# Latent attention on one core: two heads of a pair share one value product in the column halves of TensorE's array

## The chip, the cores and the metric

One core of a Trainium2 chip runs the whole program. A core has TensorE (matrix products, called PE in the profile, its weight loads PEld), VectorE (DVE), ScalarE (ACT), GpSimd (POOL) and SyncE (SP, which issues the weight DMAs); each works through its own queue in order and waits for the others on semaphores. SBUF is the working memory, PSUM the memory of eight banks that TensorE writes. The metric is the device time of one execution in microseconds (us), as a median of the runs.

## The reference

Two transformer blocks of the same sequence follow one another: a block with a feed-forward layer, a hybrid mixer and another feed-forward layer, and a second block of two layers with a recurrent mixer and a window attention. The change touches one part only, the latent attention of the mixer. It has 8 heads, 512 tokens and 16 meta tokens, and for every block of 128 queries only the keys up to its own block are used:

```python
def latent_attention(q_nope, q_rope, k_nope, k_rope, v, cid):
    scale = (MLA_NOPE + MLA_ROPE) ** -0.5
    outs = []
    for blk in range(lp // Q_BLOCK):
        q0, q1 = blk * Q_BLOCK, (blk + 1) * Q_BLOCK
        kend = min(lp, chunk_end(q1 - 1))
...
        s = s.astype(jnp.float32) * scale
        mask = cid[None, :kend] <= cid[q0:q1, None]
        p = jax.nn.softmax(jnp.where(mask, s, NEG_INF), axis=-1)
        outs.append(jnp.einsum('bhts,bhsd->bhtd', p.astype(v.dtype), v[:, :, :kend]))
    return jnp.concatenate(outs, axis=2)
```

A head's query and key have 96 elements, its value 64.

## The kernel before

The program is a list of stages; between some of them (`phase_end`) TensorE, ScalarE and VectorE wait for one another. `s_latent` is one stage. It interleaves two works that have nothing to do with each other: the latent attention, and the 16 gate projections that the mixer needs later.

**Units.** The attention is cut into `NU` = 32 units of one head and one block of 128 queries. Unit u has i + 1 blocks of 128 keys (called n = i + 1 below, 1 to 4) and the 16 meta keys. Before the change the order is head, then query block, so n runs 1, 2, 3, 4, 1, 2, 3, 4. For each unit:

- `scores` (TensorE, L1578 and L1579): one product for the n key blocks, one for the meta keys, into one of two PSUM areas (`sbank`); it waits until the exponent of the unit two before has read that area.
- `top` (VectorE, L1641, L1643, L1647): masks a corner, takes the row maximum and scales it.
- exponent (ScalarE, L1692) from PSUM into `pm`, with the row sum; two buffers.
- `norm` (VectorE, L1652, L1655): reciprocal of the sum, and `pm` scaled by it in place.
- `turn` (TensorE, L1588 and L1591): n transposes and one for the meta keys, into PSUM bank 4 and 5.
- `keep` (ScalarE, L1686 and L1687): copies the transposed probabilities into `pT`, two buffers of 640 columns.
- `pv` (TensorE, L1601 and L1603): the value product. The stationary operand is a head's value block, 128 keys by 64, the moving one 128 columns of `pT`; n products and one with the 16 meta keys add up in PSUM bank 6. The result has 64 rows: a head with an even number takes partitions 0 to 63 of the bank, one with an odd number 64 to 127.

**Gate work.** `gate(n)` is one step of a projection: three matmuls of 128 by 128 with 512 columns (L294, L295, L296 in the helper `mm3`). Eight steps fill PSUM bank 7 with one chunk; VectorE then copies it out (L1664) and ScalarE and GpSimd split the next weight chunk (L282, L289). All 16 chunks use bank 7, so the first step of a chunk waits for that copy.

**Order.** It is written out by hand. TensorE's iteration u: `scores(u + 2)`, two gate steps, `turn(u)`, a gate step, `pv(u - 1)`, a gate step. A chunk of the gates takes two iterations, so a new chunk begins in every even iteration, right after `scores`. VectorE's iteration u: `top(u + 1)`, in even ones the gate copy of the chunk that has just ended, `norm(u)`. ScalarE's: exponent of u, `keep(u - 1)`, in even ones a weight split; after both heads of a pair are done it also copies bank 6 into `ym` (L1700), which VectorE completes (L1659).

Most float32 products of the attention show as two records in the trace for one matmul of the program: `pv` of n blocks has 2n records on L1601 and two on L1603. The transposes have one each, and so have the gate steps.

Of the kernel before, what the change touches and what calls it, by code (L numbers as in the profile page):

```python
# [17 lines left out]
ACT = mybir.ActivationFunctionType  # L18
# [3 lines left out]
P = 128  # L22
T = 512
META = 16
# [62 lines left out]
def slot_of(base, k, per_body=RING, j=0):  # L87

    g = base + k
    return g % RING, g // RING + (per_body // RING) * j, g + per_body * j  # L90


def program(nc, d, out):
    with ExitStack() as ctx:
# [9 lines left out]
        def local(kind, **totals):  # L104


            out_ = []
            for i, total in enumerate(totals.values()):
                name = f"{kind}{i}"
                out_.append(Signal(sem(name).s, ends.get(name, 0)))  # L110
                ends[name] = ends.get(name, 0) + total
            return out_
# [4 lines left out]
        def at(name, off, shape, dt=F32):  # L117

            n = 4 * int(np.prod(shape[1:]))
            assert off + n <= 56800 * 4, (name, off, n)  # L120
            return nc.alloc_sbuf_tensor_at(name, shape, dt, offset=base0 + off, align_bytes=4)
# [6 lines left out]
        o_tmp = o_big + 98304  # L128
# [60 lines left out]
        vm = at("vm", B + 32768, [P, 5, 8, 64])  # L189
# [1 line left out]
        km = at("km", B + 79872, [96, 8, TK])  # L191
        ym = at("ym", B + 63488, [P, 4, 2, T], F32R)
        pm = at("pm", o_tmp, [P, 2, TK])
        pT = at("pT", o_tmp + 4224, [P, 2, 640])
        kvf = at("kvf", o_tmp + 9344, [P, 2, TK])
        st = at("st", o_tmp + 13568, [P, 64])
        mixh = at("mixh", X + 1024, [P, DT, T], F32R)
        mixl = at("mixl", X + 1024 + 4 * DT * T, [P, DT, T], F32R)
        f_mix = at("f_mix", B, [P, DT, TK])
# [46 lines left out]
        PS = ctx.enter_context(nc.psum_tensor("PS", [P, 8 * 512], F32))  # L246
        PS3 = PS[:, :].rearrange("p (b n) -> p b n", b=8)
# [5 lines left out]
        def c_(name, lo=0, hi=None, rows=slice(0, P)):  # L253
            return con[rows, COFF[name] + lo:COFF[name] + (dict(CON)[name] if hi is None else hi)]
# [46 lines left out]
        def phase_end(eng, who):  # L301

            bars[who] += 1
            eng.drain().then_inc(phase_over.s, 1)
            eng.wait_ge(*phase_over(3 * bars[who]))
# [136 lines left out]
        def xn_ready(pe, tag, t):  # L442

            if tag in raw_low:
                pe.wait_ge(*raw_low[tag](t + 1))
            else:
                pe.wait_ge(*xn_done[tag][t % 2](t // 2 + 1))
# [1101 lines left out]


        def s_latent():
            units = [(hd, i) for hd in range(8) for i in range(4)]
            NU = len(units)
            SC = float(96) ** -0.5
            s_done, masked, mx_done, nb_done, p_done, rs_done, pn_done, t_done, tc_done, pv_done = local(
                "st", s=NU, mask=NU, mx=NU, nb=NU, p=NU, rs=NU, pn=NU, t=NU, tc=NU, pv=NU)
            y_hi, y_lo = local("su", yhi=4, ylo=4)

            gate_base = BASE["gate"]
# [2 lines left out]
            def width(u):  # L1562
                return P * (units[u][1] + 1) + META

            def sbank(u, a, b, rows=slice(0, P)):
                o = 1024 * (u % 2)
                return PS[rows, o + a:o + b]

            def pe(pe):
                phase_end(pe, "pe")  # L1570

                def scores(u):
                    hd, i = units[u]
                    n = P * (i + 1)
                    if u >= 2:
                        pe.wait_ge(*p_done(u - 1))
                    q = qm[:, hd, i * P:(i + 1) * P]
                    pe.matmul(sbank(u, 0, n), q, km[:, hd, 0:n], start=True, stop=True, skip_group_check=True)  # L1578
                    pe.matmul(sbank(u, n, n + META), q, km[:, hd, T:TK], start=True, stop=True,  # L1579
                              skip_group_check=True).then_inc(s_done.s, 1)  # L1580

                def turn(u):
                    hd, i = units[u]
                    pe.wait_ge(*pn_done(u + 1))
                    if u >= 1:
                        pe.wait_ge(*tc_done(u))
                    for x in range(i + 1):
                        pe.transpose(PS[:, 2048 + x * P:2048 + (x + 1) * P], pm[:, u % 2, x * P:(x + 1) * P],  # L1588
                                  c_("ident"))
                    n = P * (i + 1)  # L1590
                    pe.transpose(PS[0:META, 2560:2560 + P], pm[:, u % 2, n:n + META], c_("ident")).then_inc(t_done.s, 1)  # L1591

                def pv(u):
                    hd, i = units[u]
                    r = 64 * (hd % 2)
                    pe.wait_ge(*tc_done(u + 1))
                    if hd >= 2 and hd % 2 == 0 and i == 0:
                        pe.wait_ge(*y_lo(hd // 2))
                    o = PS3[r:r + 64, 6, i * P:(i + 1) * P]
                    for x in range(i + 1):  # L1600
                        pe.matmul(o, vm[:, x, hd, :], pT[:, u % 2, x * P:(x + 1) * P], start=(x == 0),  # L1601
                                  stop=False, skip_group_check=True)
                    pe.matmul(o, vm[0:META, 4, hd, :], pT[0:META, u % 2, 512:640], start=False, stop=True,  # L1603
                              skip_group_check=True).then_inc(pv_done.s, 1)

                def gate(n):

                    c, kt = divmod(n, DT)
                    s, _, g = slot_of(gate_base, c)
                    if kt == 0:  # L1610
                        pe.wait_ge(*lo_done(g + 1))
                        if c:
                            pe.wait_ge(*gate_out(c))
                    if c == 0:
                        xn_ready(pe, "gx", kt)
                    ins = mm3(pe, PS3[:, 7, :], s, kt * P, (kt + 1) * P, xh512[:, kt, :], xl512[:, kt, :],
                              kt == 0, kt == DT - 1)
                    if kt == DT - 1:
                        ins.then_inc(chunk_used.s, 1)
                scores(0)  # L1620
                scores(1)
                for u in range(NU):
                    if u + 2 < NU:
                        scores(u + 2)
                    gate(4 * u)
                    gate(4 * u + 1)
                    turn(u)
                    gate(4 * u + 2)
                    if u >= 1:
                        pv(u - 1)  # L1630
                    gate(4 * u + 3)
                pv(NU - 1)

            def dve(dve):
                phase_end(dve, "dve")
# [41 lines left out]
            def act(act):  # L1677
                phase_end(act, "act")
                act.preload_act_table_set("natural_log_exp_and_others")

                def keep(u):
                    n = P * (units[u][1] + 1)
                    act.wait_ge(*t_done(u + 1))
                    if u >= 2:
                        act.wait_ge(*pv_done(u - 1))
                    act.activation(pT[0:META, u % 2, 512:640], PS[0:META, 2560:2560 + P], ACT.Copy)  # L1686
                    act.activation(pT[:, u % 2, 0:n], PS[:, 2048:2048 + n], ACT.Copy).then_inc(tc_done.s, 1)  # L1687
                for u in range(NU):
                    act.wait_ge(*nb_done(u + 1))
                    if u >= 2:  # L1690
                        act.wait_ge(*t_done(u - 1))
                    act.activation(pm[:, u % 2, 0:width(u)], sbank(u, 0, width(u)), ACT.Exp,  # L1692
                                   bias=st[:, 4 + u % 4:5 + u % 4], scale=SC,
                                   accum_out=st[:, 8 + u % 4:9 + u % 4]).then_inc(p_done.s, 1)
                    if u >= 1:
                        keep(u - 1)
                    if u % 8 == 1 and u >= 8:
                        pair = u // 8 - 1
                        act.wait_ge(*pv_done(8 * pair + 8))
                        act.activation(ym[:, pair, 0, :], PS3[:, 6, :], ACT.Copy).then_inc(y_hi.s, 1)  # L1700
                    if u % 2 == 0 and u >= 2:
                        split_hi(act, gate_base, u // 2 - 1 + 4)
                keep(NU - 1)
                split_hi(act, gate_base, 15 + 4)
                act.wait_ge(*pv_done(NU))
                act.activation(ym[:, 3, 0, :], PS3[:, 6, :], ACT.Copy).then_inc(y_hi.s, 1)
            sp_, pool_ = weights("gate")
            stage(pe, act, dve, pool_, sp_)
# [1064 lines left out]
        s_c_split()  # L2773
        s_mla_project()
        s_latent()
        led = s_mix()
        parts = s_out("wout", (8,), lambda kt, i: (mixh[:, kt, :], mixl[:, kt, :]), T, 4, led, f_mix)
# [202 lines left out]
```

## Time and profile before

| | us |
|---|---|
| median of 3 runs | 2752.3 |
| lowest, highest run | 2749.68, 2753.54 |
| the profiled execution's own time | 2752.45 |
| its span, first to last instruction | 2750.7 |
| TensorE busy (share of the span) | 2619.9 (95%) |
| VectorE, ScalarE, GpSimd busy | 1301.3, 934.3, 1002.4 |

TensorE's granted clock is 0.978 of full over the span. On the profile's page, the chain of work that ended last lies on TensorE for 84% of the span and on VectorE for 9%. Busy time on TensorE counts modelled ends of pipelined matmuls, which overlap; what a piece of work costs there is better read from the distance between starts. The stage `s_latent` runs from 692.6 to 870.4 us.

### The profile page before, as it was taken

To read this page: it belongs to the slowest core of one execution; us is meant where nothing else is said; L and a number is where in the kernel's file an instruction comes from. 1 tells how busy PE (TensorE), PEld (TensorE's weight loads), DVE (VectorE), ACT (ScalarE), POOL (GpSimd) and SP (SyncE) were. 2 spreads that over 40 slices of the span, in tenths; PEclk is the share of its full clock that TensorE was granted. 3 is DMA by queue.
4 is the path that set the end of the run, shared out by engine and by line. 5 is a ranking of instruction groups with operands and counts; after the bars stand their busy time and mean duration, and the time that the engine had idled before them with its cause. 6 is when DMAs were issued, how large, how long until landed. Compare 5 with 4: busy or idle time off the path is not lost.

```text
span 2750.7 us, 35023 instructions
## 1 busy us (share of the span) xinstructions
PE 2619.9 (95%) x13396; PEld 2145.8 (78%) x13396; DVE 1301.3 (47%) x1448; ACT 934.3 (34%) x1305; POOL 1002.4 (36%) x447
## 2 busy tenths in 40 slices
PE   7999999897999999999899899999999899999999
PEld 7999998755676778888667478888877578888887
DVE  4333113467444544430367576664146655666313
ACT  4222223373334242222344232222245453222223
POOL 4433443202222334444323134444444104444442
PEclk9999999998999999999999999999999999999999
DMA  4222232101111222223222022223322102323232
GB/s 165 91 91 75 85 108 77 48 1 41 46 47 62 79 82 99 92 82 97 83 74 77 16 90 93 99 94 105 100 84 92 46 10 99 99 92 99 100 100 69
DMA packets 65650, 219.37 MB, mean 80 GB/s; under 512 B 8273, under 2 KB 8529, under 8 KB 65426
## 3 DMA queue, kind: packets, MB, share of 16 engines
q1 hardware_dynamic: 63792, 216.60, 24.1%
q10 hardware_dynamic: 1762, 1.45, 0.2%
q8 instruction: 65, 1.06, 0.2%
q14 instruction: 31, 0.25, 0.0%
HBM read 215.92 MB, written 2.10 MB: 79 GB/s over the span
## 4 chain that ended last, share of the span: by engine, by line
PE 84%; DVE 9%; ACT 3%; issue 3%; DMA 0%; DVEq 0%; ACTq 0%; SPq 0%; POOL 0%
PE PS L294 25%; PE PS L296 25%; PE PS L295 25%; PE PS L2635 1%; DVE acc L494 1%; PE PS L1601 1%; ACT xh L468 1%; PE PS L1228 1%; PE PS L1578 1%; DVE h L564 1%; PE PS L2618 1%; DVE mt L1752 1%; DVE xl L472 1%; PE PS L1213 1%; DVE sq L486 0%
## 5 line engine op out<-in xcount | busy, mean ns | idle before, releaser
L289 POOL TENSOR_TENSOR wlo<-wraw,whi 128x1024 fp32r<-128x1024 f32 (+2 forms) x425 | 994.4, 2342 | 1560.6 <-ACT whi L282 1560.3
L294 PE MATMUL PS<-xh,whi 128*128 128x512 f32 (+2 forms) x2536 | 908.5, 358 | 44.5 <-DVE xl L472 20.0
L295 PE MATMUL PS<-xl,whi 128*128 128x512 f32 (+2 forms) x2536 | 894.5, 353 | 0.0
L296 PE MATMUL PS<-xh,wlo 128*128 128x512 f32 (+2 forms) x2536 | 894.4, 353 | 0.0
L282 ACT ACTIVATE whi<-wraw 128x1024 fp32r<-128x1024 f32 (+2 forms) x425 | 428.4, 1009 | 857.8 <-PE PS L296 855.8
L294 PEld LDWEIGHTS PS<-xh,whi 128*128 128x128 f32 (+1 forms) x2536 | 478.8, 189 | 119.0 <-issue 24.6
L296 PEld LDWEIGHTS PS<-xh,wlo 128*128 128x128 f32 (+1 forms) x2536 | 479.1, 189 | 65.7 <-issue 0.5
L295 PEld LDWEIGHTS PS<-xl,whi 128*128 128x128 f32 (+1 forms) x2536 | 479.4, 189 | 61.2 <-issue 1.4
L294 PE MATMUL PS<-hid2h,whi 128*128 128x512 f32 x560 | 217.8, 389 | 0.0
L295 PE MATMUL PS<-hid2l,whi 128*128 128x512 f32 x560 | 217.8, 389 | 0.0
L296 PE MATMUL PS<-hid2h,wlo 128*128 128x512 f32 x560 | 217.8, 389 | 0.0
L295 PEld LDWEIGHTS PS<-hid2l,whi 128*128 128x128 f32 x560 | 105.1, 188 | 22.0
L294 PEld LDWEIGHTS PS<-hid2h,whi 128*128 128x128 f32 x560 | 105.1, 188 | 21.8
L926 DVE TENSOR_TENSOR h<-PS,h 128x512 f32<-128x512 f32 x24 | 16.6, 692 | 222.9 <-PE PS L296 222.9
L296 PEld LDWEIGHTS PS<-hid2h,wlo 128*128 128x128 f32 x560 | 105.1, 188 | 21.7
L998 DVE TENSOR_SCALAR f<-PS 128x528 f32<-128x528 f32 (+1 forms) x16 | 11.2, 700 | 221.1 <-ACT sq L986 200.6
L816 DVE SCALAR_TENSOR_TENSOR gc<-gp,vec,gc 128x512 f32<-128x512 f32 x96 | 112.5, 1229 | 0.0
L295 PE MATMUL PS<-hid1l,whi 128*128 128x264 f32 x352 | 100.3, 285 | 0.0
L296 PE MATMUL PS<-hid1h,wlo 128*128 128x264 f32 x352 | 100.2, 285 | 0.0
L294 PE MATMUL PS<-hid1h,whi 128*128 128x264 f32 x352 | 100.1, 284 | 0.0
L806 DVE TENSOR_TENSOR gp<-PS,rb_up 128x1024 f32<-128x1024 f32 x24 | 29.4, 1224 | 144.8 <-PE PS L296 144.8
L468 ACT ACTIVATE xh<-h,vec 128x512 fp32r<-128x512 f32 (+1 forms) x64 | 45.6, 722 | 151.7 <-DVE h L926 112.4
(414 smaller groups left out, 3311.5 us busy)
## 6 DMA issues: line engine op xcount, KB each, us to landing
wraw<-w_up_dram SPq DMA_DIRECT2D x96, 512.0 KB, 3.4
wraw<-w_dn_dram SPq DMA_DIRECT2D x48, 512.0 KB, 3.4
wraw<-w_f1gu_dram SPq DMA_DIRECT2D x44, 512.0 KB, 3.2
wraw<-w_f2gu_dram SPq DMA_DIRECT2D x44, 512.0 KB, 3.4
wraw<-w_hyin_dram SPq DMA_DIRECT2D x24, 512.0 KB, 3.5
wraw<-w_win_dram SPq DMA_DIRECT2D x18, 512.0 KB, 3.2
wraw<-w_gate_dram SPq DMA_DIRECT2D x16, 512.0 KB, 3.2
wraw<-w_pg_dram SPq DMA_DIRECT2D x16, 512.0 KB, 3.4
```

The costliest lines, as they stand in the source:

```text
L282: act.activation(whi[:, s, 0:size], wraw[:, s, 0:size], ACT.Copy).then_inc(hi_done.s, 1)
L289: pool.tensor_tensor(wlo[:, s, 0:size], wraw[:, s, 0:size], whi[:, s, 0:size].bitcast(F32), ALU.subtract).then_inc(lo_done.s, 1)
L294: pe.matmul(out_, whi[:, s, a:b], xhi, start=start, stop=False, skip_group_check=True)
L295: pe.matmul(out_, whi[:, s, a:b], xlo, start=False, stop=False, skip_group_check=True)
L296: return pe.matmul(out_, wlo[:, s, a:b], xhi, start=False, stop=stop, skip_group_check=True)
L468: act.activation(dh[:, t, 0:n], h[:, t, 0:n], ACT.Copy, scale=v_(gain, t)).then_inc(high.s, 1)
L472: dve.scalar_tensor_tensor(dl[:, t, 0:n], h[:, t, 0:n], v_(gain, t), dh[:, t, 0:n].bitcast(F32), ALU.mult, ALU.subtract).then_inc(low.s, 1)
L494: dve.tensor_tensor(acc[:, 0:n], acc[:, 0:n], sq[:, 0:n], ALU.add).then_inc(summed.s, 1)
L564: dve.tensor_tensor(h[:, t, 0:n], scaled_f[:, t % 2, 0:n], h[:, t, 0:n], ALU.add).then_inc(kept.s, 1)
L806: dve.tensor_tensor(gp[:, :, 2:T + 2], bank(0, 2), spread(rb_up, 1), ALU.mult).then_inc(g_read.s, 1)
L816: ins = dve.scalar_tensor_tensor(gc[:, m, :], gp[:, m, tap:T + tap], vec[:, bass.ds(2 * j + (cw + FF2T * tap + m), 1)], gc[:, m, :], ALU.m ...
L1213: ins = pe.matmul(PS3[0:rows(u), 2 * (u % 3) + hd, c0:T], ks[r:r + 64, p, k0:k1], qs[r:r + 64, p, c0:T], start=True, stop=False, skip_grou ...
```

## The change

Units are ordered pair of heads, query block, head of the pair: n runs 1, 1, 2, 2, 3, 3, 4, 4. The value product `pv(m)` now serves the two units 2m and 2m + 1, which are the two heads of a pair at the same query block. Its matmuls alternate between the heads, so that each one goes to the other half of the array's columns than the one before it: partitions 0 to 63 of bank 6, then 64 to 127. It runs in every second iteration (even u from 2 on) and once at the end. `pT` has four buffers instead of two, and `st` lies further back in memory to make room. The waits and counts on `pv_done` follow; `keep(u)` now waits for the value product of units u - 4 and its pair.

```diff
-            units = [(hd, i) for hd in range(8) for i in range(4)]
+            units = [(2 * p + e, i) for p in range(4) for i in range(4) for e in range(2)]
...
-                def pv(u):
-                    hd, i = units[u]
-                    r = 64 * (hd % 2)
-                    pe.wait_ge(*tc_done(u + 1))
-                    if hd >= 2 and hd % 2 == 0 and i == 0:
-                        pe.wait_ge(*y_lo(hd // 2))
-                    o = PS3[r:r + 64, 6, i * P:(i + 1) * P]
+                def pv(m):
+                    p, i = divmod(m, 4)
+                    pe.wait_ge(*tc_done(2 * m + 2))
+                    if p >= 1 and i == 0:
+                        pe.wait_ge(*y_lo(p))
+
+                    def o(e):
+                        return PS3[64 * e:64 * e + 64, 6, i * P:(i + 1) * P]
                     for x in range(i + 1):
-                        pe.matmul(o, vm[:, x, hd, :], pT[:, u % 2, x * P:(x + 1) * P], start=(x == 0),
-                                  stop=False, skip_group_check=True)
-                    pe.matmul(o, vm[0:META, 4, hd, :], pT[0:META, u % 2, 512:640], start=False, stop=True,
-                              skip_group_check=True).then_inc(pv_done.s, 1)
+                        for e in range(2):
+                            pe.matmul(o(e), vm[:, x, 2 * p + e, :], pT[:, (2 * m + e) % 4, x * P:(x + 1) * P], start=(x == 0),
+                                      stop=False, skip_group_check=True)
+                    for e in range(2):
+                        ins = pe.matmul(o(e), vm[0:META, 4, 2 * p + e, :], pT[0:META, (2 * m + e) % 4, 512:640], start=False,
+                                        stop=True, skip_group_check=True)
+                    ins.then_inc(pv_done.s, 1)
...
-                    if u >= 1:
-                        pv(u - 1)
+                    if u >= 2 and u % 2 == 0:
+                        pv(u // 2 - 1)
                     gate(4 * u + 3)
-                pv(NU - 1)
+                pv(NU // 2 - 1)
...
-                    if u >= 2:
-                        act.wait_ge(*pv_done(u - 1))
+                    if u >= 4:
+                        act.wait_ge(*pv_done(u // 2 - 1))
```

TensorE, value products, before: the end of iteration 3 and a part of iteration 4, with value products in both (`xh_56`, `xl_57` and `whi`, `wlo` are the gate steps' operands, `pT` and `vm` those of the value product).

```order
L294 MATMUL PS<-xh_56,whi 128x512
L295 MATMUL PS<-xl_57,whi 128x512
L296 MATMUL PS<-xh_56,wlo 128x512
L1601 MATMUL PS<-pT,vm 64x128 [waits st8]
L1601 MATMUL PS<-pT,vm 64x128 x2
L1603 MATMUL PS<-pT,vm 64x128
L294 MATMUL PS<-xh_56,whi 128x512
L295 MATMUL PS<-xl_57,whi 128x512
L296 MATMUL PS<-xh_56,wlo 128x512
...
L1601 MATMUL PS<-pT,vm 64x128 [waits st8]
L1601 MATMUL PS<-pT,vm 64x128 x3
L1603 MATMUL PS<-pT,vm 64x128
```

TensorE, the same place after: iteration 4 from its third gate step on.

```order
L294 MATMUL PS<-xh_56,whi 128x512
L295 MATMUL PS<-xl_57,whi 128x512
L296 MATMUL PS<-xh_56,wlo 128x512
L1603 MATMUL PS<-pT,vm 64x128 [waits st8]
L1603 MATMUL PS<-pT,vm 64x128 x3
L1606 MATMUL PS<-pT,vm 64x128 x2
L294 MATMUL PS<-xh_56,whi 128x512
L295 MATMUL PS<-xl_57,whi 128x512
L296 MATMUL PS<-xh_56,wlo 128x512
```

Iteration 3 has no value product any more, and that of iteration 4 is for both heads of the pair at two key blocks: four matmuls and two for the meta keys, in one piece.

TensorE, before: the scores at the head of iterations 4 and 5, and the gate step behind each (the first one begins a chunk and waits for the copy of bank 7).

```order
L1578 MATMUL PS<-km,qm 128x384 [waits st4]
L1579 MATMUL PS<-km,qm 128x16
L294 MATMUL PS<-xh_56,whi 128x512 [waits gate0,lo_done]
...
L1578 MATMUL PS<-km,qm 128x512 [waits st4]
L1579 MATMUL PS<-km,qm 128x16
L294 MATMUL PS<-xh_56,whi 128x512
```

TensorE, after: the same two places.

```order
L1578 MATMUL PS<-km,qm 128x512 [waits st4]
L1579 MATMUL PS<-km,qm 128x16
L294 MATMUL PS<-xh_56,whi 128x512 [waits gate0,lo_done]
...
L1578 MATMUL PS<-km,qm 128x512 [waits st4]
L1579 MATMUL PS<-km,qm 128x16
L294 MATMUL PS<-xh_56,whi 128x512
```

In iteration 4 the scores ahead of the waiting gate step now have four key blocks, where they had three.

VectorE, before: the gate copy of iteration 6 (L1664) with the scaling of units 6 and 7 behind it.

```order
L1643 TENSOR_REDUCE st<-PS 128x1 [waits st1]
L1647 TENSOR_SCALAR st<-st 128x1 [waits st4,st2]
L1664 TENSOR_TENSOR gates<-PS,rbx 128x512 [waits chunk_used]
L1652 RECIPROCAL st<-st 128x1 [waits st4]
L1655 TENSOR_SCALAR pm<-pm,st 128x400 [waits st5]
L1641 MEMSET PS 64x64 [waits st0]
L1643 TENSOR_REDUCE st<-PS 128x1 [waits st1]
L1647 TENSOR_SCALAR st<-st 128x1 [waits st4,st2]
L1652 RECIPROCAL st<-st 128x1 [waits st4]
L1655 TENSOR_SCALAR pm<-pm,st 128x528 [waits st5]
```

VectorE, after: the same place (lines are four higher).

```order
L1647 TENSOR_REDUCE st<-PS 128x1 [waits st1]
L1651 TENSOR_SCALAR st<-st 128x1 [waits st4,st2]
L1668 TENSOR_TENSOR gates<-PS,rbx 128x512 [waits chunk_used]
L1656 RECIPROCAL st<-st 128x1 [waits st4]
L1659 TENSOR_SCALAR pm<-pm,st 128x528 [waits st5]
L1645 MEMSET PS 64x64 [waits st0]
L1647 TENSOR_REDUCE st<-PS 128x1 [waits st1]
L1651 TENSOR_SCALAR st<-st 128x1 [waits st4,st2]
L1656 RECIPROCAL st<-st 128x1 [waits st4]
L1659 TENSOR_SCALAR pm<-pm,st 128x528 [waits st5]
```

The kinds and their order are the same; the scaling behind the gate copy is four key blocks wide and was three.

## Rows read from the trace of the kernel before

**Rows 1.** Busy time by engine: the whole latent stage, then four of its units.
```profile
core 0: us, PE busy (x) PEld busy (x) DVE busy (x) ACT busy (x) POOL busy (x), PEclk, DMA share, GB/s
692.60:870.40 177.80, 171.02 (x849) 123.52 (x849) 73.68 (x180) 56.20 (x150) 37.54 (x16) 0.98 0.14 48
705.83:727.49 21.66, 21.04 (x108) 15.21 (x107) 9.01 (x22) 6.53 (x18) 4.78 (x2) 1.00 0.15 49
```

**Rows 2.** Groups of instructions on TensorE, 690 to 875 us, each shape apart.
```profile
L294 PE MATMUL PS<-xh,whi 128*128 128x512 f32 x128 | 59.4, 464 | 5.2 <-DVE gates L1664 4.5
...
L1601 PE MATMUL PS<-pT,vm 128*64 128x128 f32 x160 | 24.3, 283 | 0.0
```

**Rows 3.** Timeline, TensorE: start us, duration us; one value product, one block.
```profile
790.51 0.40 PE L296 MATMUL PS<-xh,wlo 128*128 128x512 f32 x1
...
790.84 0.43 PE L1601 MATMUL PS<-pT,vm 128*64 128x128 f32 x2
...
791.20 0.43 PE L1603 MATMUL PS<-pT,vm 16*64 16x128 f32 x2
...
791.56 0.50 PE L294 MATMUL PS<-xh,whi 128*128 128x512 f32 x1
...
791.90 0.39 PE L295 MATMUL PS<-xl,whi 128*128 128x512 f32 x1
792.13 0.40 PE L296 MATMUL PS<-xh,wlo 128*128 128x512 f32 x1
```

**Rows 4.** Timeline, TensorE: the value product of a unit with four blocks.
```profile
806.37 0.40 PE L296 MATMUL PS<-xh,wlo 128*128 128x512 f32 x1
806.69 1.09 PE L1601 MATMUL PS<-pT,vm 128*64 128x128 f32 x8
...
808.41 0.39 PE L295 MATMUL PS<-xl,whi 128*128 128x512 f32 x1
```

**Rows 5.** Timeline, TensorE: value products of the other two attentions.
```profile
585.04 0.44 PE L1249 MATMUL PS<-aa,vs 128*64 128x128 f32 x4
585.41 0.33 PE L1228 MATMUL PS<-sph,cr 128*128 128x128 f32 x1
...
2198.38 0.65 PE L2650 MATMUL PS<-apt,va 128*64 128x256 f32 x4
2198.97 0.49 PE L2618 MATMUL PS<-kdup,qa 64*128 64x256 f32 x2
...
2206.57 1.08 PE L2650 MATMUL PS<-apt,va 128*64 128x256 f32 x8
2207.58 0.49 PE L2618 MATMUL PS<-kdup,qa 64*128 64x256 f32 x2
```

**Rows 6.** Timeline, TensorE: scores of one block and of four, next gate matmul.
```profile
792.36 0.39 PE L1578 MATMUL PS<-km,qm 96*128 96x128 f32 x2
...
793.40 0.47 PE L294 MATMUL PS<-xh,whi 128*128 128x512 f32 x1 [0.52 <-DVE gates L1664]
...
852.10 1.02 PE L1578 MATMUL PS<-km,qm 96*128 96x512 f32 x2
...
853.11 0.48 PE L294 MATMUL PS<-xh,whi 128*128 128x512 f32 x1
```

**Rows 7.** Timeline, all engines: scalings near a weight split; the last unit's copy.
```profile
793.36 0.43 DVE L1655 TENSOR_SCALAR pm<-pm,st 128x400 f32<-128x400 f32 x1
...
793.76 2.40 POOL L289 TENSOR_TENSOR wlo<-wraw,whi 128x1024 fp32r<-128x1024 f32 x1 [8.40 <-ACT whi L282]
...
794.60 1.85 DVE L1655 TENSOR_SCALAR pm<-pm,st 128x528 f32<-128x528 f32 x1
...
794.86 0.49 PE L1588 MATMUL PS<-con,pm 128*128 128x128 f32 x3
...
864.54 0.48 PE L294 MATMUL PS<-xh,whi 128*128 128x512 f32 x1
...
864.99 0.57 ACT L1687 ACTIVATE pT<-PS 128x512 f32<-128x512 f32 x1
```

More of the change, by code:

```diff
@@ L193, in program @@
         pm = at("pm", o_tmp, [P, 2, TK])
-        pT = at("pT", o_tmp + 4224, [P, 2, 640])
+        pT = at("pT", o_tmp + 4224, [P, 4, 640])
         kvf = at("kvf", o_tmp + 9344, [P, 2, TK])
-        st = at("st", o_tmp + 13568, [P, 64])
+        st = at("st", o_tmp + 14464, [P, 64])
         mixh = at("mixh", X + 1024, [P, DT, T], F32R)
@@ L1555, in s_latent @@
             s_done, masked, mx_done, nb_done, p_done, rs_done, pn_done, t_done, tc_done, pv_done = local(
-                "st", s=NU, mask=NU, mx=NU, nb=NU, p=NU, rs=NU, pn=NU, t=NU, tc=NU, pv=NU)
+                "st", s=NU, mask=NU, mx=NU, nb=NU, p=NU, rs=NU, pn=NU, t=NU, tc=NU, pv=NU // 2)
             y_hi, y_lo = local("su", yhi=4, ylo=4)
@@ L1683, in keep @@
                     act.wait_ge(*t_done(u + 1))
-                    if u >= 2:
-                        act.wait_ge(*pv_done(u - 1))
-                    act.activation(pT[0:META, u % 2, 512:640], PS[0:META, 2560:2560 + P], ACT.Copy)
-                    act.activation(pT[:, u % 2, 0:n], PS[:, 2048:2048 + n], ACT.Copy).then_inc(tc_done.s, 1)
+                    if u >= 4:
+                        act.wait_ge(*pv_done(u // 2 - 1))
+                    act.activation(pT[0:META, u % 4, 512:640], PS[0:META, 2560:2560 + P], ACT.Copy)
+                    act.activation(pT[:, u % 4, 0:n], PS[:, 2048:2048 + n], ACT.Copy).then_inc(tc_done.s, 1)
                 for u in range(NU):
@@ L1698, in act @@
                         pair = u // 8 - 1
-                        act.wait_ge(*pv_done(8 * pair + 8))
+                        act.wait_ge(*pv_done(4 * pair + 4))
                         act.activation(ym[:, pair, 0, :], PS3[:, 6, :], ACT.Copy).then_inc(y_hi.s, 1)
@@ L1704, in act @@
                 split_hi(act, gate_base, 15 + 4)
-                act.wait_ge(*pv_done(NU))
+                act.wait_ge(*pv_done(NU // 2))
                 act.activation(ym[:, 3, 0, :], PS3[:, 6, :], ACT.Copy).then_inc(y_hi.s, 1)
```

## The prediction

> **What bounds the kernel now.** I read the busy times by engine over the stage first. In its 177.80 us TensorE is busy for 171.02, VectorE for 73.68, ScalarE for 56.20, GpSimd for 37.54, and the clock is at 0.98 of full; a run of four units takes 21.66 us, TensorE busy for 21.04 of it, at full clock [rows 1]. So TensorE sets the pace, and whatever leaves its queue leaves the time, as long as nothing else comes late. The groups show what of that time is the value product: 160 records of L1601 with a mean of 283 ns [rows 2], and two of L1603 behind each unit's. The durations contain the pipeline; what the product takes from the queue I read from the starts in the timeline [rows 3, 4]. The only idle time of weight in the stage is before the gate steps, 5.2 us, of which 4.5 us wait for VectorE's copy of bank 7 [rows 2].
>
> **What one value product costs.** Two gate matmuls that follow one another start 0.23 us apart (791.90, 792.13) [rows 3]. Around the product of a unit with one key block, the last gate matmul before it starts at 790.51 and the second one after it at 791.90: 1.39 us, of which 0.46 would be there anyway, so 0.93 us [rows 3]. With four blocks it is 808.41 - 806.37 - 0.46 = 1.58 us [rows 4]. That is (1.58 - 0.93) / 3 = 0.22 us for each further matmul of 128 columns, so 1.15 and 1.36 for two and three blocks. The product with one block has two matmuls (data and meta), 0.44 us, and thus a fixed 0.49 us: entering it, going over to the 16-row operand, going back, and a gate matmul after it that starts late. Summed over n = 1 to 4 it is 0.93 + 1.15 + 1.36 + 1.58 = 5.02, times 8 heads 40.2 us.
>
> **Two heads at once.** The trace of before has no latent value product in both column halves, but it has two other attentions whose value products alternate halves. In the first, four records of 128 columns with a stationary operand of the same 128x64 shape (two matmuls, one for each head) take from 585.04 to 585.41, 0.37 us [rows 5]; one matmul of that shape in the latent stage takes 791.20 - 790.84 = 0.36 us to its successor [rows 3]. In the second, going from four records to eight (a further pair of 256 columns) moves the successor from 0.59 to 1.01 us: 0.42 us for two matmuls [rows 5], where at 0.22 for each 128 columns they would take 0.88 in one half. So both halves work at the same time and a pair costs what one did. I take that, and 0.01 us on top at each of the two kinds of operand: 16 products of the new kind cost 16 x 0.02 = 0.3 us more than 16 old ones.
>
> Sum: 40.2 / 2 = 20.1 us removed (half of the matmul time and half of the fixed parts), 0.3 added: **19.8 us**.
>
> A rule speaks against this. The Trainium skill, TensorE: Matmul & The Clock Gate, Part 3 (What overlaps and what doesn't), says that a weight load overlaps with a matmul in flight only when the row groups differ. The two heads use the same rows, so by that rule the halves would not run side by side; the rows of the two other attentions disagree. What it would leave is rival A.
>
> Bounds: those rows don't show long runs of pairs at 128 columns, where four weight loads fall into 0.22 us. If only the first pair of each kind overlaps, the 0 + 1 + 2 + 3 further pairs of the four sizes, times 4, cost 0.22 more each: 24 x 0.22 = 5.3 us. Below the 0.37 us of a pair no row goes.
>
> **The order of the units.** In an even iteration a new gate chunk begins behind the scores, and waits for bank 7's copy. Counted from the start of the scores, the gate step starts 793.40 - 792.36 = 1.04 us later with one block; four blocks pass in 853.11 - 852.10 = 1.01 us without a wait [rows 6]. A block is 0.21 us of L1578 (128 columns in two records), so one, two and three blocks pass in 0.37, 0.58 and 0.79, and the waits are 0.67, 0.46, 0.25 and, for four, 0.03 us. Before, the scores in even iterations have one block 7 times and three blocks 7 times: 4.7 + 1.8 = 6.5 us. After, they have 1, 2, 3, 4 blocks 3, 3, 4, 4 times: 2.0 + 1.4 + 1.0 + 0.1 = 4.5 us. The last even iteration has no scores on either side. Gain **1.9 us**. Against it stands the start: the scores of unit 1 lose one block, and since TensorE then waits for unit 0's exponent, that block's 0.2 us is not made up; cost **0.2 us**.
>
> **Waits that move.** `pv(m)` waits for the `keep` of unit 2m + 1, which follows that unit's transposes, an iteration earlier: as far as before. At the end `pv(15)` comes two gate steps after the last transposes: the first began at 864.54, so the second was through at 864.54 + 6 x 0.23 = 865.9, and the copy for it ended at 864.99 + 0.57 = 865.56 [rows 7]; those steps hide it with 0.3 us to spare, and without them it would cost about a microsecond, once. `keep(u)` waits for a value product two iterations old or more, and behind it on ScalarE only the exponent could be held up, which it isn't. The wait of the next pair for bank 6 (`y_lo`) has an iteration more than before. The scores, transposes, copies and DMAs are the same in number, and so is the buffer move: nothing. The weight chunks of the gates come due 11% faster, with GpSimd busy for 37.54 of 177.80 us [rows 1]: no wait.
>
> VectorE's scaling of an even unit stands behind the gate copy and ahead of the transposes. With three blocks it ran from 793.36 for 0.43 us, the transposes started at 794.86, and GpSimd's split at 793.76 [rows 7]. Units with four blocks now stand there too, four times; with a third more work it ends at 793.94, 0.9 us early. I price this at nothing; rival B says when it isn't.
>
> **Forecast.** 19.8 + 1.9 - 0.2 = 21.5 us off the profiled execution's own 2752.45 gives 2730.95. Its time and the median of 2752.3 differ by 0.15, so the same holds for the median: **2731 us**, 0.8% less.
>
> **Rivals.**
> A. The halves don't overlap. Then only 16 of the fixed parts go: 16 x 0.49 = 7.8, with the order's 1.7 it is 9.5 us, 2743.0. For it: nothing in the rows, only the rule named above. Against: both rows of the other attentions. A part of it is the bound above, overlap in first pairs alone: 2736.3.
> B. VectorE's scaling is caught by GpSimd. The scaling of the odd unit, begun at 794.60 while the split ran (793.76 to 796.16), took 1.85 us and ended 0.3 after it, against 0.43 for the narrower one begun ahead of it [rows 7]. Should the four-block scaling of an even unit fare like this, it ends at about 796.45 instead of 793.94, and the transposes due at 794.86 start 1.6 us later, 4 times: 6.6 us, 2737.5. Against: it begins 0.4 us ahead of the split, as the narrower one did.
> C. Slower: every change of half drains the array. Where one matmul must end before the next of the other half begins, the gap is its duration, 0.283 [rows 2], instead of 0.11 us, 0.17 more. A product with n blocks has 2n + 1 changes; over the 16 it is 4 x (3 + 5 + 7 + 9) = 96, so 16.3 us over rival A: 2759.3. It decides from 9.5 / 96 = 0.10 us for a change on. Against: the pairs in the other attentions, which change halves as often.
> The Trainium skill, TensorEngine Tiling (Array Packing), Key Properties, has a drain for a change of the tiling mode and not for one of the tile; that too speaks against C.
> D. The change doesn't do what it says: the matmuls are issued alternately on the queue, so this leaves only a wait that I don't see. Each of the 15 value products inside the loop held up by 1 us would make 2746.
>
> **Chances.** Forecast 0.72; partial overlap 0.07; B 0.07; A 0.08; C 0.03; D 0.03. The range takes in the forecast, the partial overlap and B, with some microseconds for the spread of the runs (2749.68 to 2753.54): **2726 to 2740**. A measurement can tell about 0.2% (5.5 us) from no change: faster by more than that is everything but C and most of D, 0.94; within it 0.03; slower 0.03.
>
> **What the profile after would show.** Right: value products of n blocks that take, from the last gate matmul before to the second after, 0.95 to 1.6 us for both heads; four L1603 and four L1606 records in 0.7 us for one block; a stage of about 156 us; eight units in 38 us; waits for bank 7 after one-block scores three times only. Rival A would show 0.22 us more for each matmul, B scalings of 2 us in even units with idle time ahead of L1588, C record distances of 0.28 us. A time outside of the range with the stage at 156 us would mean that a later stage took or gave it.

## The result and the profile after

| | before | after |
|---|---|---|
| median, us (6 runs each) | 2752.6 | 2729.1 |
| lowest to highest | 2746.33 to 2753.54 | 2725.73 to 2730.52 |
| profiled execution's own time | 2752.45 | 2726.47 |
| its span | 2750.7 | 2724.8 |
| latent stage, first score matmul to the next stage's first matmul | 692.61 to 870.37: 177.76 | 693.90 to 849.80: 155.90 |
| span less that stage | 2572.94 | 2568.90 |

The ratio of the times is 0.9917, with a 95% interval of 0.9906 to 0.9928: 23.5 us less, where 21.5 were forecast (2731.0, in a range of 2726 to 2740). The stage alone became 21.86 us shorter.

Busy times by engine over the stage, to be read against [rows 1] (columns: stretch, its length, busy time and count of TensorE, its weight loads, VectorE, ScalarE, GpSimd, then clock, DMA share, GB/s):

```profile
693.90:849.80 155.90, 150.16 (x849) 113.46 (x849) 71.99 (x180) 56.05 (x150) 37.49 (x16) 0.98 0.17 55
```

TensorE still has nearly all of the time. The counts of instructions are what they were. The groups of TensorE in the stage (against [rows 2]; the value product is now L1603 for the key blocks and L1606 for the meta keys):

```profile
L294 PE MATMUL PS<-xh,whi 128*128 128x512 f32 x128 | 57.6, 450 | 3.8 <-DVE gates L1668 3.4
...
L1603 PE MATMUL PS<-pT,vm 128*64 128x128 f32 x160 | 12.3, 283 | 0.0
...
L1606 PE MATMUL PS<-pT,vm 16*64 16x128 f32 x64 | 6.9, 293 | 0.0
```

Still 160 records with a mean of 283 ns for the key blocks, but together they cover 12.3 us where they covered 24.3. The busy time counts a moment once, so twice as many matmuls run at once; the mean of one record says nothing of it.

Timeline of TensorE, a value product of one block, now for two heads (against [rows 3]):

```profile
708.63 0.40 PE L296 MATMUL PS<-xh,wlo 128*128 128x512 f32 x1
...
708.96 0.44 PE L1603 MATMUL PS<-pT,vm 128*64 128x128 f32 x4
...
709.33 0.43 PE L1606 MATMUL PS<-pT,vm 16*64 16x128 f32 x4
...
709.70 0.50 PE L294 MATMUL PS<-xh,whi 128*128 128x512 f32 x1
...
710.03 0.39 PE L295 MATMUL PS<-xl,whi 128*128 128x512 f32 x1
```

From the last gate matmul before to the second after it is 710.03 - 708.63 = 1.40 us, less the 0.46 of two gate matmuls 0.94, for both heads; one head took 0.93. With four blocks (against [rows 4]):

```profile
737.01 0.40 PE L296 MATMUL PS<-xh,wlo 128*128 128x512 f32 x1
...
737.33 1.09 PE L1603 MATMUL PS<-pT,vm 128*64 128x128 f32 x16
...
738.36 0.43 PE L1606 MATMUL PS<-pT,vm 16*64 16x128 f32 x4
...
739.06 0.39 PE L295 MATMUL PS<-xl,whi 128*128 128x512 f32 x1
```

739.06 - 737.01 - 0.46 = 1.59 us for both heads, 16 records, where one head took 1.58 with 8.

Timeline of three engines in an even iteration, unit 6, with scores of one block ahead of the gate step that waits (against [rows 6, 7]):

```profile
724.25 0.38 PE L1578 MATMUL PS<-km,qm 96*128 96x128 f32 x2
...
725.25 0.50 DVE L1659 TENSOR_SCALAR pm<-pm,st 128x528 f32<-128x528 f32 x1
...
725.29 0.47 PE L294 MATMUL PS<-xh,whi 128*128 128x512 f32 x1 [0.52 <-DVE gates L1668]
...
725.64 2.39 POOL L289 TENSOR_TENSOR wlo<-wraw,whi 128x1024 fp32r<-128x1024 f32 x1 [7.37 <-ACT whi L282]
...
726.49 1.83 DVE L1659 TENSOR_SCALAR pm<-pm,st 128x528 f32<-128x528 f32 x1
...
726.75 0.60 PE L1588 MATMUL PS<-con,pm 128*128 128x128 f32 x4
```

The gate step starts 725.29 - 724.25 = 1.04 us after the scores, as before. VectorE's scaling of four blocks ran from 725.25 for 0.50 us and ended after GpSimd's split had begun at 725.64, without being held; the scaling of the odd unit, begun behind the split, took 1.83.

### The profile page after: what moved, and what is told of

The parts are those of the page before. It is cut to its first block, busy times and chain, and to the rows that moved or that the text cites. A ratio compares the mean times of both kernels' runs of the same rounds, so it can differ in the third digit from the quotient of the medians.

```text
span 2724.8 us, 35021 instructions
## 1 busy us (share of the span) xinstructions
PE 2598.2 (95%) x13396; PEld 2136.7 (78%) x13396; DVE 1298.5 (48%) x1448; ACT 934.1 (34%) x1305; POOL 1001.7 (37%) x447
## 4 chain that ended last, share of the span: by engine, by line
PE 85%; DVE 9%; issue 3%; ACT 3%; DMA 0%; DVEq 0%; ACTq 0%; POOL 0%; SPq 0%
PE PS L294 25%; PE PS L296 25%; PE PS L295 25%; PE PS L2639 1%; DVE acc L494 1%; ACT xh L468 1%; PE PS L1228 1%; DVE mt L1756 1%; PE PS L1578 1%; DVE h L564 1%; PE PS L2622 1%; DVE xl L472 1%; PE PS L1213 1%; DVE sq L486 0%; DVE qkf L1783 0%
```

## The experiments

All stage lengths below are read like those of the table, from the first score matmul to the first matmul of the next stage. They are sharper than the times of whole runs: two profiles of the changed kernel give 155.90 and 155.94, while span less stage differs by up to 4 us from profile to profile.

They have one blur of their own, the granted clock at the stage's border, ahead of which TensorE sits idle for 3.0 us. Six profiles (before, after and its repetition, the order alone, one head after the other, the early product) enter the stage at a granted clock of 0.50, the 1.2 GHz level, and are back at full clock after 6.0 us. The other four (both heads in one half, halves changed after every second matmul, the early product with 128 partitions, the kernel before with the early product) have 0.69 to 0.71 over the first 2 us, since the clock falls only about 0.8 us into the stage, and are back 7.6 us in. They come to the same instruction about 0.5 us later. This is the first score matmul and the first value product of the changed kernel, then of the one with both heads in one half, whose programs are equal up to there (in brackets the idle time before it and who ended it; DVEq is VectorE's queue):

```profile
693.90 0.79 PE L1578 MATMUL PS<-km,qm 96*128 96x128 f32 x2 [2.98 <-DVEq L304]
...
708.96 0.44 PE L1603 MATMUL PS<-pT,vm 128*64 128x128 f32 x4
```

```profile
690.32 0.49 PE L1578 MATMUL PS<-km,qm 96*128 96x128 f32 x2 [2.98 <-DVEq L304]
...
705.95 0.65 PE L1603 MATMUL PS<-pT,vm 128*64 128x128 f32 x4
```

The first scores are faster at full clock (0.49 against 0.79), but then TensorE waits longer for unit 0's exponent and does more of the work behind it at half clock: 15.63 us to the product against 15.06. Where two kernels of different kinds are compared below, 0.5 us of the difference is the clock.

**The order of the units alone.** The kernel before, with

```diff
-            units = [(hd, i) for hd in range(8) for i in range(4)]
+            units = [(2 * p + e, i) for p in range(4) for i in range(4) for e in range(2)]
```

> The kernel before with the new order of the units and nothing else: every unit still has its own value product. My theory: only the waits for bank 7's copy change, 7 x 0.67 + 7 x 0.25 to 3 x 0.67 + 3 x 0.46 + 4 x 0.25 + 4 x 0.03, less 0.2 at the start: 1.7 us faster than before, about 2751. If the order were what brings most of the changed kernel's gain it would be near 2730.

Measured: 2750.12 us against 2751.24 of before (ratio 0.9995, 0.9986 to 1.0004), the stage 693.93 to 869.74, 175.81: 1.95 us less than before, with 1.7 expected. The waits of its stage (total us, times, longest):

```profile
PE PS L294 <- DVE gates L1664: 3.4, 7, 0.9
```

Before it was 4.5 us, 8 times, and 3.4, 7 times, is also what the changed kernel has. The rows count only the part of a wait in which no earlier matmul is still running, so the term has to be read from starts. The order by itself brings nothing that whole runs could tell.

**Both heads in one half.** The changed kernel with both heads' results in partitions 0 to 63; the odd head's half stays without its values.

```diff
-                        return PS3[64 * e:64 * e + 64, 6, i * P:(i + 1) * P]
+                        return PS3[0:64, 6, i * P:(i + 1) * P]
```

> The changed kernel, but both heads of a pair go to partitions 0 to 63 of bank 6 (the odd head's result is left out of its place), in the same alternating order. My theory: without a second half nothing overlaps, 0.22 us for each of 4 x (2+3+4+5) = 56 matmuls: 12.3 us slower than the changed kernel, 2741. Rival: the gain comes from alternating two products, whatever the half: 2729.

Measured: 2741.61 us (0.9965 of before, 0.9951 to 0.9978); the stage 690.32 to 858.75, 168.43, 12.53 us longer than after. A value product of four blocks:

```profile
736.22 1.96 PE L1603 MATMUL PS<-pT,vm 128*64 128x128 f32 x16
738.11 0.65 PE L1606 MATMUL PS<-pT,vm 16*64 16x128 f32 x4
738.68 0.50 PE L294 MATMUL PS<-xh,whi 128*128 128x512 f32 x1
```

From the first record to the meta keys it is 1.89 us (1.03 in the changed kernel), from there to the gate step 0.57 (0.36). Of the 12.53 us, 0.57 (15.63 - 15.06) is the clock at the stage's start, so 12.0 us are the two halves at work together, and alternating two products in one half brings none of it. Against the order alone, this kernel joins two products into one and saves 175.81 - 168.43 = 7.38 us, and 7.9 when the clock's 0.5 is given back: the fixed parts. One rival has no run: here both heads also add into the same place of PSUM, and not only into the same half. Against it speak the transposes, each of which writes to a place of its own and which still start 0.11 us apart, record by record (736.31 and 736.42 us in the changed kernel), as the records of a value product in one half do.

**One head after the other.** The changed kernel with the loops of the key blocks exchanged:

```diff
-                    for x in range(i + 1):
-                        for e in range(2):
+                    for e in range(2):
+                        for x in range(i + 1):
```

> The changed kernel, but inside a value product all matmuls of the even head's key blocks come first, then all of the odd head's, then the two for the meta keys. My theory: the halves overlap only where the two heads' matmuls are neighbours. The key-block matmuls no longer do (0.22 us for each of 4 x (1+2+3+4) = 40): 8.8 us slower than the changed kernel, or somewhat less for the one neighbouring pair of each product, 2734.5 to 2738. Rival: TensorE runs the halves beside each other without regard to the order (a queue for each half): 2729.

Measured: 2732.59 us (0.993 of before, 0.9914 to 0.9945); the stage 693.80 to 852.72, 158.92, only 3.02 us longer than after. Both expectations miss. Products of three and of four blocks:

```profile
727.98 1.15 PE L1603 MATMUL PS<-pT,vm 128*64 128x128 f32 x12
...
729.05 0.43 PE L1606 MATMUL PS<-pT,vm 16*64 16x128 f32 x4
...
737.52 1.58 PE L1603 MATMUL PS<-pT,vm 128*64 128x128 f32 x16
...
739.04 0.43 PE L1606 MATMUL PS<-pT,vm 16*64 16x128 f32 x4
```

To the meta keys it is 729.05 - 727.98 = 1.07 us for three blocks and 1.52 for four; the changed kernel takes 0.81 and 1.03. For one and two blocks there is no difference (0.37 and 0.59). So (0.26 + 0.49) x 4 = 3.0 us, the whole of it. Less the 0.15 of the change to the meta keys' rows and in units of 0.22, three and three took 4.2 matmul times and four and four 6.2: the two heads run together for about two matmuls of each, 3 + 3 - 2 and 4 + 4 - 2, and not only for the one pair of neighbours. The single records, which the timeline merges, show it directly. With four blocks one chain of eight records, 0.11 us apart, starts at 737.53, and a second one at 738.02, together with the fifth record of the first, so that it runs beside the first one's last four (two matmuls). With three blocks the second chain starts at 728.25, again beside the last four records of the first. The records don't name their head, but two chains at once can only be the two heads: matmuls of the odd head start before matmuls of the even head that stand ahead of them in the program. In the changed kernel the records of the two halves start in pairs, 0.01 us apart, and the pairs 0.11 us apart.

**Change of halves after every second matmul.** The order of two and two, to test that reading.

```diff
-                    for x in range(i + 1):
-                        for e in range(2):
+                    for x, e in sorted(((x, e) for x in range(i + 1) for e in range(2)),
+                                       key=lambda t: (t[0] // 2, t[1], t[0])):
+                        if True:
```

> The changed kernel, but the matmuls of a value product change halves after every second one of the key blocks (even, even, odd, odd), not after every one. My theory after e2_grouped, where three and three took 0.26 and four and four 0.49 us longer than alternating and two and two nothing: TensorE begins a matmul of the other half up to two matmuls ahead of its turn. Then this order costs nothing: stage 155.9. Rival: each run of equal halves costs a part of a matmul: for three and four blocks 0.1 to 0.2 us more each, the stage 157 to 158.

Measured, one run: 2729.96 us, the stage 692.32 to 849.06, 156.74. Its product of four blocks:

```profile
736.31 1.14 PE L1604 MATMUL PS<-pT,vm 128*64 128x128 f32 x16
737.39 0.43 PE L1607 MATMUL PS<-pT,vm 16*64 16x128 f32 x4
```

1.08 us to the meta keys, 0.05 more than in turn; that of three takes the same 0.81. The products therefore cost 4 x 0.05 = 0.2 us more. Of the other 0.6 us of the stage, 0.55 had come before its first value product (15.61 us after the first scores, against 15.06), where the two programs are the same: the clock at the stage's start again. So up to two matmuls of the other half are nearly free to come early; that it is two matmuls, or four records, and not a time, these runs don't tell apart.

**The value product ahead of the waiting gate step.**

```diff
+                    if u >= 2 and u % 2 == 0:
+                        pv(u // 2 - 1)
                     gate(4 * u)
                     gate(4 * u + 1)
                     turn(u)
                     gate(4 * u + 2)
-                    if u >= 2 and u % 2 == 0:
-                        pv(u // 2 - 1)
```

> The changed kernel with the value product of an even iteration moved from behind the third gate step to right behind the scores, ahead of the gate step that waits for bank 7's copy. My theory: a value product takes 0.93 to 1.58 us and scores 0.37 or more, together over the 1.04 us that the copy takes, so it covers all waits for bank 7, 4.5 us and 1.0 in the last even iteration: 5.5 us faster than the changed kernel, 2723.5. Rival: it then waits for ScalarE's copy of the last transposes, and the wait is only moved: 2729.

Measured: 2722.05 us (0.9895 of before, 0.988 to 0.991); the stage 691.63 to 840.74, 149.11: 6.79 us less than after, with 5.5 expected. Iteration 6 of TensorE, the same place as the one above with the wait:

```profile
721.54 0.39 PE L1578 MATMUL PS<-km,qm 96*128 96x128 f32 x2
721.76 0.29 PE L1579 MATMUL PS<-km,qm 96*128 96x16 f32 x2
721.99 0.88 PE L1603 MATMUL PS<-pT,vm 128*64 128x128 f32 x12
722.79 0.43 PE L1606 MATMUL PS<-pT,vm 16*64 16x128 f32 x4
723.16 0.50 PE L294 MATMUL PS<-xh,whi 128*128 128x512 f32 x1
...
723.96 0.40 PE L294 MATMUL PS<-xh,whi 128*128 128x512 f32 x1
```

The product starts 0.23 us behind the last scores and the gate step right behind the product, and no wait for bank 7 is left in the stage's list. The 1.3 us that were not expected fit a second effect: a gate step behind scores pushes the next one back a little (in the changed kernel the one that starts at 725.29 has the next at 726.06, 0.77 us later, where three gate matmuls take 0.69), and one behind a value product does so too. With the product between scores and gate, there is one such place less in an iteration: 15 x 0.08 = 1.2 us.

**The same place in the kernel before.** Its own value product of every unit moved right behind the scores, with nothing of the change.

```diff
+                    if u >= 1:
+                        pv(u - 1)
                     gate(4 * u)
                     gate(4 * u + 1)
                     turn(u)
                     gate(4 * u + 2)
-                    if u >= 1:
-                        pv(u - 1)
```

> The kernel before with its own value product, unit for unit, moved right behind the scores in every iteration. My theory: it covers the waits for bank 7 (7 x 0.67 + 7 x 0.25 + 1.03 = 7.5 us) and saves about 0.08 us at each entry as in e4_early (31 of them, 2.5): stage 177.76 - 10 = 167.8, time about 2742. Rival: with one head less between the transposes and the product it waits for ScalarE's copy instead: the stage at 172 or more.

Measured: 2740.26 us against 2752.52 (0.9955, 0.9938 to 0.9972); the stage 691.88 to 859.43, 167.55, as expected. An odd iteration of it:

```profile
715.43 0.81 PE L1578 MATMUL PS<-km,qm 96*128 96x384 f32 x2
716.08 0.29 PE L1579 MATMUL PS<-km,qm 96*128 96x16 f32 x2
716.30 1.09 PE L1601 MATMUL PS<-pT,vm 128*64 128x128 f32 x8
717.32 0.43 PE L1603 MATMUL PS<-pT,vm 16*64 16x128 f32 x2
717.67 0.50 PE L294 MATMUL PS<-xh,whi 128*128 128x512 f32 x1
```

The stage became 177.76 - 167.55 = 10.2 us shorter, or 10.7 with the clock's 0.5 given back (unit 3's scores start 8.58 us into the stage, 8.08 in the kernel before, with the same work ahead of them). That is the sum of the 7.5 us of waits and the 2.5 us of entries; how it divides between the two, this run doesn't tell. So about half of what the change brings (10.2 of 21.9 us in the stage) was to be had by moving two lines.

**Meta keys on all 128 partitions.** On top of the early product; the partitions without meta keys are zeroed, once, in both operands.

```diff
-                        ins = pe.matmul(o(e), vm[0:META, 4, 2 * p + e, :], pT[0:META, (2 * m + e) % 4, 512:640], start=False,
+                        ins = pe.matmul(o(e), vm[:, 4, 2 * p + e, :], pT[:, (2 * m + e) % 4, 512:640], start=False,
...
+                    if hd == 0:
+                        ch.link(dve.memset(vm[:, 4, :, :], 0.0))
...
+                Chain(dve, "dve_chain").link(dve.memset(pT[:, :, 512:640], 0.0))
```

> The kernel with the early value product (e4_early), and the meta keys' matmuls take all 128 partitions, of which the 112 that hold no meta keys are set to zero beforehand. My theory: of the fixed part of a value product 0.14 us is the change from 128-row to 16-row operands; with it gone the stage is 16 x 0.14 = 2.2 us shorter than the 149.11 of e4_early: 146.9, and the time about 2720. Rival: the gap between key blocks and meta keys isn't the row count but the fill of a new group, and stays: 149.1.

Measured: 2721.26 us against 2752.52 (0.9886, 0.9869 to 0.9902); the stage 693.68 to 841.07, 147.39, 1.72 us less than with the early product alone. Its product of four blocks:

```profile
733.15 1.09 PE L1605 MATMUL PS<-pT,vm 128*64 128x128 f32 x16
734.07 0.39 PE L1608 MATMUL PS<-pT,vm 128*64 128x128 f32 x4
734.39 0.50 PE L294 MATMUL PS<-xh,whi 128*128 128x512 f32 x1
```

0.92 us to the meta keys instead of 1.03, and 0.32 from there to the gate step instead of 0.36: 0.15 of each product was the change of rows, or 2.4 us in 16. Of that the stage lost 0.7 again. 0.5 of it is the clock at the stage's start: the first value product starts 12.87 us after the first scores, 12.36 in the early kernel. With that given back the gain is 2.2 us, as expected; the other 0.2 of the 2.4 stay open. Whole runs can't tell this kernel from the early one. Both medians are 7 to 8 us under the changed kernel's, and this one's is the lowest measured.

**The changed kernel again.**

> The changed kernel again, beside the others on the same chip: stage 155.9, time 23 us under before. If the gain outside of the stage in the first profile (4 us) was of the change, span less stage is again near 2568.9; if it is the spread from run to run, it may be anywhere from 2568 to 2573.

Measured: 2729.13 us against 2752.52 (0.9916, 0.99 to 0.9933); the stage 690.95 to 846.89, 155.94, and span less stage 2568.96. By the rule written beforehand that speaks for a part of the gain outside of the stage. The other profiles speak against: of the kernels with the change, span less stage is 2572.5 with one head after the other, 2571.3 with both in one half, 2571.5 with two and two, 2569.7 and 2571.7 with the early product; of those without it, 2572.8 with the order alone and 2570.6 in the kernel before with the early product. Nor does the shortfall lie in one place. From the stage's end to the last gating of the mixer (VectorE, `mt`) it is 51.0 to 51.3 us in all of them. From the first scores of the last stage, the window attention, to the end it is 568.3 or 568.4 in every kernel. The first score matmul of the latent stage starts anywhere from 690.3 to 693.9, and from the mixer to the window attention it is 1255.6 to 1261.4 (1255.6 in the first profile of after, 1258.6 in this one, 1260.8 in before); the granted clock over this stretch is 0.97 in the three profiles where it is longest and 0.98 in the others, so a part of the spread goes with the clock. The changed kernel's two low sums thus come from two different stretches, neither of which the change touches. I take the 4 us for spread and count the stage's 21.9; with the medians' 23.5 less 21.9, 1.6 us stay within the interval.

## Why the prediction was right

Term by term, with what the runs gave for each:

| | forecast, us | measured in the stage, us |
|---|---|---|
| order of the units, with the start | 1.9 - 0.2 = 1.7 | 1.95 (order alone) |
| fixed parts of 16 products gone | 16 x 0.49 = 7.8 | 7.38 (one half against order alone); 7.9 with the clock set right |
| two halves at once | 56 x 0.22 - 0.3 = 12.0 | 12.53 (after against one half); 12.0 with the clock set right |
| sum | 21.5 | 21.86 |

The profile of the kernel with one half is of the kind that is 0.5 us slower at the stage's start, which moves as much from the second term to the third and leaves the sum alone, since before and after are of the same kind. The measured sum is that of the stage; the medians' other 1.6 us had no term in the forecast, and no run gives them a cause.

- What bounds the stage held: TensorE, with nothing new that came late. None of the waits that the change moved (`keep`, `y_lo`, the last product, the weight chunks) appears in its list of waits of a matmul: beside the stage's borders that has only those for bank 7 and, once, the one for unit 0's exponent, 0.5 us, where before had 0.1. That wait is not itself the price: the order alone starts unit 3's scores 7.83 us into the stage, 0.25 ahead of before (8.08), with two blocks of scores fewer behind it, which are 0.44 us at full clock. So the start cost 0.2, as forecast.
- The step with the greatest weight, that a pair costs what one did, was taken from two other attentions of the same kernel, with fewer matmuls or wider ones. It held at 128 columns and up to four pairs in a row: 0.94 and 1.59 us for both heads. The partial overlap priced as a bound did not come: the 32 weight loads and matmuls of four pairs passed in 1.03 us.
- Rival A (halves don't overlap) and C (every change of halves drains) are out by the same rows; the kernel with both heads in one half shows what A would have been, 2741.6 where 2743.0 was forecast for it. The rule of the Trainium skill's page TensorE: Matmul & The Clock Gate, Part 3, that a weight load overlaps with a matmul in flight only when the row groups differ, is not what these runs show for two column halves in the same rows. Nor does it hold where the whole array is used: in [rows 1] matmuls are busy for 171.02 and weight loads for 123.52 of 177.80 us, so they overlap for at least 116 (the ends of matmuls are modelled), and nearly all of them use all or most of the rows. So the rule gave no good reason for rival A.
- Rival B (scaling held by GpSimd) did not come: the scaling begun at 725.25, 0.39 us ahead of the split, took 0.50. The other half of its reasoning is right, since the one begun behind the split took 1.83. Its price of 6.6 us is a slip of little weight: 4 x 1.6 is 6.4.
- The waits for bank 7 came as worked out: 1.04 us from the scores for one block, 3.4 us in the list where 4.5 stood. But they were listed as a side term of 1.9 us, and the greater part of them was left standing; the early product took 6.8 us more, of which the forecast says nothing.

## What to carry to other kernels

When a product fills half of the array's columns and another one like it exists, put both in one instruction group in different column halves; price it from any place in the same trace that already does so, by distances of starts and not by mean durations. Every separate visit with another operand shape has a fixed cost (0.49 us here, of which 0.15 was the change from 128 to 16 rows), so fewer and longer visits gain even without overlap. Before reading tenths of a us from a comparison of two profiles, look whether both entered the stage at the same granted clock. And before working on what the busiest engine computes, look at what it has waiting in its queue that could stand ahead of a wait: moving two lines was worth half of this change in the kernel before.

## What the runs showed of the hardware

- Matmuls in different column halves don't have to be neighbours to run together: with three and three or four and four in a row, about two matmuls of each side still overlapped (4.2 and 6.2 matmul times instead of 6 and 8), and with two and two in turn nearly all (1.08 against 1.03 us for four blocks). The single records of the second half start beside the last four of the first (738.02 and 728.25 in the kernel with one head after the other).
- A memset of unused partitions to keep the row count of the operands at 128 cut 0.15 us from each visit of TensorE (0.11 going to the meta keys, 0.04 going back).
- A gate step behind scores of another shape pushes the gate step after it back by 0.08 us (0.77 us for three gate matmuls, where 0.69 is usual). That a short visit between the two shares this cost fits the early product's 1.3 us beyond its waits, and is not shown by itself.
- At the start of the latent stage, behind the same 3.0 us of idle time, TensorE's granted clock was already 0.50 in six profiles and fell only about 0.8 us later in four. The stage was 0.5 us quicker with the early fall, which lies in part in the idle time.
